# Cross-attention keys: the high weights stream both halves of the memory in one 512-column pass, and VectorE copies the keys out

## The reference, cut to what matters

```
def hybrid_mixer(x, ...):
    ...
    h = head_norm(h, ml_g, ML_HEADS).astype(x.dtype)
    return jnp.concatenate([att, h], axis=-1) @ w_out

def memory_attention(x, mem, wq, wkv, wo):
    B, S, _ = x.shape
    L = mem.shape[1]
    q = (x @ wq).reshape(B, S, XA_HEADS, XA_HD)
    kv = (mem @ wkv).reshape(B, L, 2, XA_HEADS, XA_HD)
    k, v = kv[:, :, 0], kv[:, :, 1]
    ...
```

## Time and profile before

| | us |
|---|---|
| median of 3 runs | 1162.56 (1161.37 to 1162.63) |
| the profiled execution | 1161.91 |
| its span in the trace | 1160.1 |
| TensorE busy | 1146.1 (99% of the span) |
| VectorE busy | 572.6 (49%) |
| ScalarE busy | 422.8 (36%) |
| granted clock, mean of the span | 0.998 |

### The profile page before, as it was taken

How to read it: one execution, slowest core, us unless ns; L and a number is a source line. 1 busy time by engine, 2 the same in 40 slices (tenths; PEclk the granted TensorE clock), 3 DMA queues, 4 the chain that set the end, 5 groups by cost and what they waited for, 6 DMA issues and landing times.

```text
span 1160.1 us, 14690 instructions
## 1 busy us (share of the span) xinstructions
PE 1146.1 (99%) x5454; PEld 955.7 (82%) x5454; DVE 572.6 (49%) x931; ACT 422.8 (36%) x690; POOL 33.4 (3%) x50
## 2 busy tenths in 40 slices
PE   8999999999999999999999999999999999999997
PEld 7888888888888888788898888889888888888885
DVE  4533333353338588764894765467333333343325
ACT  4412212232325377643463554345122122143222
POOL 2000000000001011000000000000000000000000
PEclk9999999999999999999999999999999999999999
DMA  7633223233222222342253341233322322332201
GB/s 256 239 94 103 93 93 104 92 110 108 91 90 73 91 71 82 99 150 73 73 166 108 106 149 55 73 109 128 106 93 90 103 96 90 102 116 91 97 30 73
DMA packets 33709, 120.86 MB, mean 104 GB/s; under 512 B 3917, under 2 KB 3933, under 8 KB 33409
## 3 DMA queue, kind: packets, MB, share of 16 engines
q1 hardware_dynamic: 30672, 109.07, 28.6%
q0 software_dynamic: 2992, 11.19, 2.8%
HBM read 118.13 MB, written 2.11 MB: 104 GB/s over the span
## 4 chain that ended last, share of the span: by engine, by line
PE 95%; DVE 3%; ACT 1%; issue 1%; DMA 0%; SPq 0%; DVEq 0%; ACTq 0%
PE ps L452 30%; PE ps L454 30%; PE ps L453 30%; PE ps L469 1%; PE ps L679 1%; PE ps L700 1%; PE ps L767 1%; DMA raw<-in_units 0%; PE ps L751 0%; DVE lg L1566 0%; PE ps L672 0%; PE ps L671 0%; PE ps L863 0%; DVE qs L1521 0%; ACT ew L927 0%
## 5 line engine op out<-in xcount | busy, mean ns | idle before, releaser
L1360 DVE TENSOR_TENSOR wlo<-raw,whi 128x1024 fp32r<-128x1024 f32 x196 | 239.7, 1227 | 372.2 <-ACT whi L927 371.3
L452 PE MATMUL ps<-xth,whi 128*128 128x512 f32 (+1 forms) x916 | 353.7, 386 | 1.7 <-DVE wlo L1492 1.7
L454 PE MATMUL ps<-xth,wlo 128*128 128x512 f32 (+1 forms) x916 | 351.6, 384 | 0.0
L453 PE MATMUL ps<-xtl,whi 128*128 128x512 f32 (+1 forms) x916 | 351.5, 384 | 0.0
L927 ACT ACTIVATE whi<-raw 128x1024 fp32r<-128x1024 f32 (+2 forms) x204 | 206.9, 1036 | 154.5 <-PE ps L454 141.8
L452 PEld LDWEIGHTS ps<-xth,whi 128*128 128x128 f32 x916 | 172.2, 188 | 35.1 <-DVE wlo L1492 2.2
L454 PEld LDWEIGHTS ps<-xth,wlo 128*128 128x128 f32 x916 | 172.1, 188 | 34.3
L453 PEld LDWEIGHTS ps<-xtl,whi 128*128 128x128 f32 x916 | 172.2, 188 | 32.9
L452 PE MATMUL ps<-whi,hhi 128*128 128x512 f32 x480 | 187.9, 391 | 0.7 <-DVE hlo L1367 0.7
L454 PE MATMUL ps<-whi,hlo 128*128 128x512 f32 x480 | 186.9, 389 | 0.0
L453 PE MATMUL ps<-wlo,hhi 128*128 128x512 f32 x480 | 186.8, 389 | 0.0
(11 more groups left out here) (186 smaller groups left out, 991.4 us busy)
## 6 DMA issues: line engine op xcount, KB each, us to landing
raw<-in_units SPq DMA_DIRECT2D x203, 512.0 KB, 3.3
gb<-in_ln_g POOLq DMA_DIRECT2D x4, 512.0 KB, 4.2
gb<-in_ln_b POOLq DMA_DIRECT2D x4, 512.0 KB, 5.4
xn<-in_x POOLq DMA_DIRECT2D x4, 512.0 KB, 12.6
wb<-in_bias_by_key POOLq DMA_DIRECT2D x8, 256.0 KB, 2.9
out<-xn SPq DMA_DIRECT2D x8, 256.0 KB, 2.0
gsp<-g_rows POOLq DMA_DIRECT2D x1, 1024.0 KB, 5.0
memn<-in_mem_cols POOLq DMA_DIRECT2D x1, 1024.0 KB, 5.6
```

The lines of the kernel that those rows point to most:

```text
L452: mm(dst, lh, rh, start=start, stop=False)
L453: mm(dst, lh, rl, start=False, stop=False)
L454: return mm(dst, ll, rh, start=False, stop=stop)
L1360: v.tensor_tensor(wlo[c % SPL][:, :], raw[c % RAW][:, :], whi[c % SPL][:, :].bitcast(F32), ALU.subtract).then_inc(lo_done, 1)
```

## The change

`mth` and `mtl` become two halves of one tile `mhl`, side by side for every k. For each k `mem_key(t)` makes two passes in place of three: the high weights past all 512 columns of `mhl` (high half of the memory to columns 0 to 255 of the bank, low half to columns 256 to 511), then the low weights past the 256 columns of the high half, added to columns 0 to 255. The two halves of the bank then have to be summed. `key_tile(t)` moves from ScalarE to VectorE, where a `tensor_reduce` over pairs (column m and column m + 256) writes `km[:, t]`. The waits stay: TensorE still waits on `xk_ev`, which VectorE now counts.

```diff
@@ -213,8 +213,8 @@
         vx = at("vx", [P, NB, MH, P + 1], ar + 82 * KB)
         grow = at("grow", [MH, S], ar + 82 * KB + NB * MH * (P + 1) * 4)
         wg = at("wg", [P, KT, 64 + GW], ar + 82 * KB, F32R)
-        mth = at("mth", [P, KT, MB * P], ar + 32 * KB, F32R)
-        mtl = at("mtl", [P, KT, MB * P], ar + 40 * KB, F32R)
+        mhl = at("mhl", [P, KT, 2 * MB * P], ar + 32 * KB, F32R)
+        mth, mtl = mhl[:, :, 0:MB * P], mhl[:, :, MB * P:]
         km = at("km", [P, KT, MB * P], ar + 48 * KB)
         kmh = at("kmh", [P, KT, MB * P], gb_at, F32R)
         kml = at("kml", [P, KT, MB * P], ar + 48 * KB, F32R)
@@ -775,10 +775,15 @@
                 elif t >= 2:
                     pe.wait_ge(xk_ev, t - 1)
                 need(U_XK + t)
-                for half in range(2):
-                    if t == 0:
-                        pe.wait_ge(mlo_done, half + 1)
-                    cols_part(U_XK + t, ps[6 + t % 2][:, 0:MB * P], mth, mtl, 4 * half, 4 * half + 4)
+                u = U_XK + t
+                for k in range(KT):
+                    if t == 0 and k % 4 == 0:
+                        pe.wait_ge(mlo_done, k // 4 + 1)
+                    c = slice(k * P, (k + 1) * P)
+                    mm(ps[6 + t % 2][:, :], whi[u % SPL][:, c], mhl[:, k, :], start=k == 0, stop=False)
+                    last = mm(ps[6 + t % 2][:, 0:MB * P], wlo[u % SPL][:, c], mth[:, k, :],
+                              start=False, stop=k == KT - 1)
+                last.then_inc(unit_used, 1)
 
 
             for h in range(MH):
@@ -1215,10 +1220,6 @@
                 act.wait_ge(mem_in, 16)
                 fn(mth[:, 4 * b:4 * b + 4, :], memn[:, 4 * b:4 * b + 4, :], ACT.Copy).then_inc(mhi_done, 1)
 
-            def key_tile(t):
-                act.wait_ge(unit_used, U_XK + t + 1)
-                fn(km[:, t, :], ps[6 + t % 2][:, 0:MB * P], ACT.Copy).then_inc(xk_ev, 1)
-
 
             weights(0, 0)
             weights(0, 1)
@@ -1268,21 +1269,17 @@
             weights(3, 1)
             for t in range(2):
                 split(U_XK + t + AHEAD)
-                key_tile(t)
             weights(3, 2)
             weights(3, 3)
             split(U_XK + 2 + AHEAD)
-            key_tile(2)
             act.preload_act_table_set("natural_log_exp_and_others")
             head_std(0, MH - 1)
             for t in range(3, 5):
                 split(U_XK + t + AHEAD)
-                key_tile(t)
             split_mt(1, 0)
             split_mt(1, 1)
             for h in range(MH - 1):
                 split(U_XK + 5 + h + AHEAD)
-                key_tile(5 + h)
                 mt_copy(h)
                 if h < 2:
                     split_mt(1, 2 + h)
@@ -1714,6 +1711,12 @@
                     .then_inc(mlo_done, 1)
 
 
+            def key_tile(t):
+                dve.wait_ge(unit_used, U_XK + t + 1)
+                pair = ps[6 + t % 2][:, :].rearrange("p (a m) -> p m a", a=2)
+                v.tensor_reduce(km[:, t, :], pair, AXX, ALU.add).then_inc(xk_ev, 1)
+
+
             weigh(0, 0)
             weigh(0, 1)
             add_part(AH - 1)
@@ -1761,25 +1764,32 @@
             silu(7)
 
             split(U_XK + AHEAD)
+            key_tile(0)
             split(U_XK + 1 + AHEAD)
             weigh(3, 0)
             weigh(3, 1)
+            key_tile(1)
             gated(2)
             weigh(3, 2)
             weigh(3, 3)
             split(U_XK + 2 + AHEAD)
             for h in range(MH - 1):
                 head_norm(h)
+                if h == 0:
+                    key_tile(2)
                 if h < 2:
                     split(U_XK + 3 + h + AHEAD)
+            key_tile(3)
             gated(MH - 1)
             split_mt(1, 0)
             split_mt(1, 1)
             for h in range(MH - 1):
                 split(U_XK + 5 + h + AHEAD)
+                key_tile(4 + h)
                 if h < 2:
                     split_mt(1, 2 + h)
             head_norm(MH - 1)
+            key_tile(KT - 1)
             mt_down(1)
 
             def key_lo(half):
```

## The result

The changed kernel takes **1175.1 us** (median of 6 runs, 1172.09 to 1176.87) against 1162.1 before (median of 6, 1161.37 to 1162.63): a ratio of 1.0108 with a 95% interval of 1.0096 to 1.0120, 13.0 us or 1.1% slower. The profiled execution took 1176.87 us.

The account below looks back on a forecast made before the run. TensorE bounds the kernel, but VectorE is full in the key stretch: 3.96 old queue + 4.8 sums + 0.1 tail + 3.2 ScalarE waits - 0.1 slack + 0.05 handover = 12.0 us, on 1162.56 giving 1174.6; range 1171.0 to 1178.5.

Parts of the forecast that it names:

- What bounds the kernel: Whole page: TensorE busy 99%; in the 36 us key stretch VectorE is full where the change adds work.
- The passes: Key tiles: a 512 and a 256 pass take 0.347 us; 0.10 us saved per tile, 0.83 for eight at most.
- The sums: VectorE's eight reduces out of PSUM: 0.69 us each until the result, 0.60 of the engine.
- The places: VectorE's queue: sums stand behind other chains' work, TensorE waits for that too; even sums costing nothing leave 8.4 us.
- the replay: Key stretch: the three engines' queues re-timed with the sums added, every other duration and distance kept; gives 12.0 us.
- The round trip: Tiles 6 and 7: VectorE waits for ScalarE, itself waiting for TensorE's transposes: 2.4 + 0.3 + 0.5 = 3.2 us.
- The clock: Rival: after new TensorE pauses of 3.5 and 3.9 us the clock falls to 1.2 GHz; 1176.6 to 1182; chance 0.10.
- signs of being wrong: Projection before 610, reduces over 0.8 us, granted clock under 1.00 after 597, or a later stretch where TensorE catches up.
- The number: Whole kernel: 12.0 us added to the 1162.56 median of three runs, forecast 1174.6 us.
- Not slower: Rival: VectorE's added 4.8 us falls into its 9.29 us hole, only the passes count: 1161.7 us; chance 0.04.
- a dearer reduce: Rival: VectorE's sums read pairs 1 KB apart at half rate, 1.13 us each on the engine: 1177.8; chance 0.09.
- a milder queue: Rival: the trip through ScalarE does not bite or the sum is cheap, leaving 8.4 to 10.4: 1171.0 to 1173.0; chance 0.11.

Follow-up runs that it names:

- pass_only: Kernel before with only the merged passes; ScalarE copies columns 0 to 255 as before, halves not summed: 1161.53 us against 1162.13.
- filler: The change with TensorE's idle time before tile 5, tile 6 and the projection filled by identity products: 1173.69 us, ratio 1.0084 to 1.0115.
- same_again: The changed kernel run once more, unaltered, beside the other kernels: 1176.56 us, ratio to before 1.0115 to 1.0146.
- pool_add: The change's merged passes, but ScalarE copies all 512 columns to staging and GpSimd adds the halves: 1162.29 us against 1161.64 before.
- places: The change with its eight sums at better places in VectorE's queue, the work the same: 1169.43 us, ratio to before 1.0052 to 1.0086.

## Why the prediction was right, point by point

**What bounds the kernel.** Right. VectorE is full in the key stretch, and the work that the change puts there comes out as TensorE's waiting time, although the page shows VectorE at 49%.

**The passes.** A pair took 0.347 to 0.353 us where 0.347 was taken. That the gain lies inside new waits fits the change, where nearly every shortened tile stands in front of a wait; no run isolates it there. That it would be 0.83 by itself was too much: pass_only shows 0.26, since tiles 0 to 3 stand in front of a wait, for ScalarE's first copy or for VectorE's `pt`.

**The sums.** 0.684 us each for 0.69, and 0.60 of the engine for 0.60. The next operation starts 0.08 before this one ends, as the splits and gains did before. The prediction set this against the Trainium skill (VectorE: DVE Perf Modes, section "The DRAIN you can't avoid"), but it left out that section's own exception: an operation that is not held starts earlier. The rows do not speak against the section.

**The places.** The forecast of the pauses against the profile of the change: tile 2 1.6 and 1.44, tile 4 1.3 and 0.99, tile 5 3.5 and 3.33, projection 3.9 and 3.66. Tile 6 was to wait 2.9 and did not, since tile 5 and its transposes ended some 3 us later than the 603.7 of the replay. The filler, with the clock at 1.00, gives 12.13 for the sum of 12.0. The claim that sums of no cost would still leave 8.4 is borne out by 9.03: each copy of 16 columns still holds VectorE for 0.08 us (585.08 to 585.16), 0.6 in all.

**The round trip.** 3.2 us of waiting for ScalarE were forecast. With the clock at 1.00 (filler) it is 2.44 + 0.25 + 0.46 = 3.15, at the forecast places. In the profile of the change it is 1.27 + 0.26 + 0.69 + 0.25 + 1.29 = 3.8, with the first of it moved to the hlo in front because tile 5 was late. Taking it out gave 12.1 - 8.8 = 3.3.

**The clock.** This is the step that went otherwise. I gave it one chance in ten, and it fell in both profiles of the change and, by the mean granted clock, in all ten executions. A granted clock under 1.00 after 597 us was one of my signs of being wrong, and it came. The price was read rightly for the second pause (2 us; here 12 matmuls at 0.427 in place of 0.227, 2.5 in all) and too high for the first. Tile 5 took twice its time, but it used up the pause in front of tile 6, and only 0.8 us of it arrived at the projection (12.94 against 12.13). Together 3.3 us in the profiled execution, and 1.6 in that of same_again, whose kind is the more frequent.

**The number.** That the median lies only 0.5 over the forecast of 1174.6 is partly luck. The delay of 12.0 was right (12.13 at the full clock). Three smaller errors nearly cancelled. I started from 1162.56, the median of three runs, where six give 1162.1: 0.5 too high. I left out the lower clock, some 1.6 us in the more frequent executions. And I left out that some time comes back at the very end.

**Not slower, a dearer reduce, a milder queue.** None came. Up to TensorE's last matmul nothing is given back: it waits once more for 0.7 us for `hlo` as before, and the delay there is 15.7. Behind it something is: from the start of the last matmul to the end of the span are 8.4 us before, 7.7 in pass_only and pool_add, and 7.2 in the change and in all the kernels that open the projection late. What sets this end was not looked into.

## What to carry to other kernels

An average share of 49% says nothing about the engine that is to take the work. Look at the stretch, and there at whether any row has an idle time in front of it. When a release of the bound engine moves into another engine's queue, price everything that stands in front of it and not its own length: here 9 of 12 us stayed when the work was all but gone, and better places for the same work took 6 away. Merging matmul passes that stream the same number of columns saved only what each pass costs beside its columns, 0.013 us, which did not pay for an operation on a full engine. And a pause of a few microseconds on TensorE can be dearer than it is long, because the work behind it ran at half the clock here. Last, look at the granted clock of every execution before taking one profile for the typical one.

## What the runs showed of the hardware

- Around idle times of 2.77 to 3.66 us on TensorE the granted clock fell to 0.50 for stretches of 3.4 or 6.8 us, in the same kernel once the one and once the other. A 512-column pass then holds the engine for 0.427 us and a 256-column one for 0.21. With the idle times cut to 1.44 us and less by useless products it stayed at 1.00. In places, where the longest idle time is 1.96 us, it nevertheless fell twice for 3.4 us, so the length of one pause is not all that counts. What else does was not tried. Two windows of places:

```profile
604.00:609.00 5.00, 4.82 (x20) 3.90 (x19) 5.00 (x8) 0.14 (x1) 0.00 (x0) 0.66 0.30 105
611.00:616.00 5.00, 5.00 (x16) 3.91 (x16) 1.45 (x4) 0.00 (x0) 0.00 (x0) 0.66 0.37 126
```

- A `tensor_reduce` over pairs 1 KB apart in PSUM, 512 numbers in and 256 out, takes 684 ns, as much as a plain two-input operation of 512 (0.68 to 0.69 us). No cost of the stride shows.
- One GpSimd add of 256 columns, 0.74 us at other moments, lasted 4.36 us in the middle of VectorE's two-input operations.
